# Expert blocks of a hierarchical MoE step: transposes issued one by one between dense products, and results copied out of PSUM by ScalarE

## What is computed

```python
def expert_block(args):
    e, tok = args
    xb = x_pad[tok]                                              # (128, 1024)
    hmid = jax.nn.silu(xb @ w_gate[e]) * (xb @ w_up[e])          # (128, 512)
    return hmid @ w_down[e]                                      # (128, 1024)
```

## Time and profile before

| | us |
|---|---|
| median of 3 runs | 1564.78 (1563.38 to 1565.76) |
| the profiled execution, its time | 1563.39 |
| the profiled execution, its span | 1561.7 |
| expert stage in it, from its first product to the last copy of `yb` | about 912 to 1510 |
| PE busy over the span | 1437.0 (92%) |
| DVE busy | 1076.0 (69%) |
| ACT busy | 783.5 (50%) |
| POOL busy | 555.0 (36%) |
| granted TensorE clock, mean | 0.956 |

### The profile page before, as it was taken

One profiled execution on the slowest core, in us unless ns is written; L12 is line 12 of the kernel. 1 busy time (PEld: TensorE's weight loads), 2 busy tenths in 40 slices (PEclk: granted clock), 3 DMA queues, 4 the chain that ended last, 5 costly groups with the idle time before them and its releaser, 6 DMA issues. The chain is left out here.

```text
span 1561.7 us, 22591 instructions
## 1 busy us (share of the span) xinstructions
PE 1437.0 (92%) x7667; PEld 1246.8 (80%) x7667; DVE 1076.0 (69%) x1414; ACT 783.5 (50%) x1053; POOL 555.0 (36%) x363
## 2 busy tenths in 40 slices
PE   5899999999999998899999559999999999999955
PEld 3899999999999997788777457788888888887842
DVE  4588823166665564544554559999999999999936
ACT  5342223233333433443342418777777777777814
POOL 5423324454444442484554013423333241111111
PEclk8999999999999999899999669999999999999978
DMA  4123332234444445677553639999999999999867
GB/s 176 42 70 96 110 116 83 79 110 156 152 151 154 146 142 188 237 222 238 164 172 111 222 142 368 391 385 382 384 374 375 381 373 378 371 378 372 312 240 292
DMA packets 166995, 360.59 MB, mean 231 GB/s; under 512 B 20948, under 2 KB 50644, under 8 KB 166932
## 3 DMA queue, kind: packets, MB, share of 16 engines
q1 hardware_dynamic: 151364, 321.85, 57.6%
q0 software_dynamic: 15568, 37.87, 7.1%
HBM read 316.00 MB, written 59.64 MB: 241 GB/s over the span
## 5 line engine op out<-in xcount | busy, mean ns | idle before, releaser
L61 PE MATMUL bank<-xh,wh 128*128 128x352 f32 x864 | 295.6, 342 | 5.7 <-ACT raw L885 2.9
L63 PE MATMUL bank<-xh,wl 128*128 128x352 f32 x864 | 279.2, 323 | 0.0
L62 PE MATMUL bank<-xl,wh 128*128 128x352 f32 x864 | 278.7, 323 | 0.0
L1801 POOL DMA_INDIRECT scratch_picked<-yb,dst x32 | 90.9, 2841 | 250.0 <-DVE yb L1974 250.0
L1887 ACT CAST wg_h<-wg 128x1024 fp32r<-128x1024 f32 x124 | 131.1, 1058 | 96.7 <-PE bank L63 61.5
L1980 DVE TENSOR_TENSOR wg_l<-wg,wg_h 128x1024 fp32r<-128x1024 f32 x128 | 156.6, 1223 | 24.8 <-ACT wu_h L1888 23.3
L61 PEld LDWEIGHTS bank<-xh,wh 128*128 128x128 f32 x864 | 163.7, 190 | 10.3 <-issue 5.5
L1639 POOL TENSOR_TENSOR wol<-wo,woh 128x1024 fp32r<-128x1024 f32 x48 | 122.0, 2553 | 126.9 <-ACT woh L972 126.8
L62 PEld LDWEIGHTS bank<-xl,wh 128*128 128x128 f32 x864 | 164.2, 190 | 2.9 <-issue 1.9
L63 PEld LDWEIGHTS bank<-xh,wl 128*128 128x128 f32 x864 | 163.2, 189 | 0.0
L1981 DVE TENSOR_TENSOR wu_l<-wu,wu_h 128x1024 fp32r<-128x1024 f32 x128 | 155.7, 1216 | 0.0
(11 more groups left out here) (382 smaller groups left out, 3259.6 us busy)
## 6 DMA issues: line engine op xcount, KB each, us to landing
wg<-in_w_gate SPq DMA_DIRECT2D x128, 512.0 KB, 6.0
wu<-in_w_up SPq DMA_DIRECT2D x128, 512.0 KB, 11.1
wd<-in_w_down SPq DMA_DIRECT2D x128, 512.0 KB, 11.0
wo<-in_w_out SPq DMA_DIRECT2D x48, 512.0 KB, 4.6
w<-in_w_in_tiles SPq DMA_DIRECT2D x36, 512.0 KB, 4.3
yy<-scratch_picked SPq DMA_DIRECT2D x8, 1024.0 KB, 14.2
scratch_xb<-stage POOLq DMA_DIRECT2D x10, 512.0 KB, 4.0
xb<-scratch_xb SPq DMA_DIRECT2D x8, 640.0 KB, 4.4
```

The costliest lines, as they stand in the source:

```text
L61: nc.tensor.matmul(acc, lh, rh, start=start, stop=False)
L62: nc.tensor.matmul(acc, lh, rl, start=False, stop=False)
L63: return nc.tensor.matmul(acc, ll, rh, start=False, stop=stop)
L1801: pool.indirect_dma_start(out=S["picked"], out_offset=bass.IndirectOffsetOnAxis(ap=dst[:], axis=0), in_=yb[:], in_offset=None, bounds_chec ...
```

## The change

`turn_x` and `turn_hid` are cut into steps of one transpose. Inside the loop `down` takes one transpose of the next x after each of its eight groups of three products, and `gate_up` takes one transpose of the previous block's `hid` after each of its first four groups of six. The order of the loop is now `gate_up(i)` with `turn_hid` of block i - 1 inside it, and `down(i - 1)` with `turn_x` of block i + 1 inside it. Outside the loop the transposes of blocks 0 and 1 and of the last `hid` stay in one row. `unload_y` moves from DVE to ACT, where it stands between `high_down(i)` and `high_hid(i)`.

```diff
@@ -1813,16 +1813,24 @@
 
         @block.tensor
         def _(pe):
-            def turn_x(i):
-                pe.wait_ge(xg_loaded, i * 16 + 16)
-                for half in range(2):
+            def turn_x_step(i, k):
+                half, q = k // 4, k % 4
+                if k == 0:
+                    pe.wait_ge(xg_loaded, i * 16 + 16)
+                if q == 0:
                     wait(pe, xT_done, i * 2 + (half - 1))
-                    for q in range(4):
-                        last = nc.tensor.transpose(bank[4 + half][:, q * P:(q + 1) * P], xg[:, (4 * half + q) * P:(4 * half + q + 1) * P],
-                                                   C["ident"][:])
-                    last.then_inc(xT_psum, 1)
-
-            def gate_up(i):
+                out = nc.tensor.transpose(bank[4 + half][:, q * P:(q + 1) * P], xg[:, k * P:(k + 1) * P], C["ident"][:])
+                if q == 3:
+                    out.then_inc(xT_psum, 1)
+
+            def turn_hid_step(i, f):
+                if f == 0:
+                    pe.wait_ge(hid_ready, i + 1)
+                out = nc.tensor.transpose(bank[6][:, f * P:(f + 1) * P], hid[:, f * P:(f + 1) * P], C["ident"][:])
+                if f == FF // P - 1:
+                    out.then_inc(hT_psum, 1)
+
+            def gate_up(i, turn_hid_of=None):
                 wait(pe, hid_ready, i)
                 for k in range(KT):
                     if k % 2 == 0:
@@ -1834,14 +1842,10 @@
                                              start=(k == 0), stop=(k == KT - 1))
                     if k % 2:
                         last.then_inc(gu_used, 1)
-
-            def turn_hid(i):
-                pe.wait_ge(hid_ready, i + 1)
-                for f in range(FF // P):
-                    last = nc.tensor.transpose(bank[6][:, f * P:(f + 1) * P], hid[:, f * P:(f + 1) * P], C["ident"][:])
-                last.then_inc(hT_psum, 1)
-
-            def down(i):
+                    if turn_hid_of is not None and k < FF // P:
+                        turn_hid_step(turn_hid_of, k)
+
+            def down(i, turn_x_of=None):
                 pe.wait_ge(hT_done, i + 1)
                 wait(pe, y_done, i * 2)
                 for f in range(FF // P):
@@ -1850,8 +1854,10 @@
                         s = slice(n * 512, (n + 1) * 512)
                         last = split_product(nc, bank[2 + n][:, :], (hT_h[:, f, :], hT_l[:, f, :]), (wd_h[:, f, s], wd_l[:, f, s]),
                                              start=(f == 0), stop=(f == FF // P - 1))
-                    last.then_inc(down_used, 1)
-
+                        if n == 1:
+                            last.then_inc(down_used, 1)
+                        if turn_x_of is not None:
+                            turn_x_step(turn_x_of, 2 * f + n)
 
             pe.wait_ge(placed, 1)
             for a in range(N_ASG):
@@ -1862,18 +1868,18 @@
             nc.tensor.matmul(bank[1][0:1, 0:MAXBLK], blk_col[:], C["ident"][0:MAXBLK, 0:MAXBLK], start=True, stop=True).then_inc(blk_psum, 1)
             pe.wait_ge(rows_ready, 1)
             m = blocks_but_three(pe) + 1
-            turn_x(0)
+            for k in range(KT):
+                turn_x_step(0, k)
             gate_up(0)
-            turn_x(1)
-            turn_hid(0)
+            for k in range(KT):
+                turn_x_step(1, k)
             with pe.Fori(1, m + 1) as i:
-                gate_up(i)
-                turn_x(i + 1)
-                down(i - 1)
-                turn_hid(i)
-            gate_up(m + 1)
+                gate_up(i, turn_hid_of=i - 1)
+                down(i - 1, turn_x_of=i + 1)
+            gate_up(m + 1, turn_hid_of=m)
             down(m)
-            turn_hid(m + 1)
+            for f in range(FF // P):
+                turn_hid_step(m + 1, f)
             down(m + 1)
 
         @block.scalar
@@ -1910,23 +1916,33 @@
                 wait(act, down_used, i * 4)
                 nc.scalar.copy(hT_h[:], bank[6][:].rearrange("p (k t) -> p k t", k=4)).then_inc(h_high, 1)
 
+            def unload_y(i):
+                wait(act, y_stored, i * 16)
+                act.wait_ge(down_used, i * 4 + 4)
+                for n in range(2):
+                    nc.scalar.copy(yb[:, n * 512:(n + 1) * 512], bank[2 + n][:, :]).then_inc(y_done, 1)
+
             high_x(0)
             m = blocks_but_three(act) + 1
 
-            def block_of(i):
+            def block_of(i, first=False):
                 high_gate_up(i + 1, range(3))
                 silu(i)
                 high_x(i + 1)
                 high_gate_up(i + 1, range(3, 4))
                 high_down(i)
+                if not first:
+                    unload_y(i - 1)
                 high_hid(i)
 
-            block_of(0)
+            block_of(0, first=True)
             with act.Fori(1, m + 1) as i:
                 block_of(i)
             silu(m + 1)
             high_down(m + 1)
+            unload_y(m)
             high_hid(m + 1)
+            unload_y(m + 1)
 
         @block.vector
         def _(dve):
@@ -1967,12 +1983,6 @@
                 wait(dve, hT_psum, i)
                 nc.vector.tensor_tensor(hid[:], act_g[:], bank[1][:, :], ALU.mult).then_inc(hid_ready, 1)
 
-            def unload_y(i):
-                wait(dve, y_stored, i * 16)
-                dve.wait_ge(down_used, i * 4 + 4)
-                for n in range(2):
-                    nc.vector.tensor_copy(yb[:, n * 512:(n + 1) * 512], bank[2 + n][:, :]).then_inc(y_done, 1)
-
             def low_gate_up(i, pieces):
                 for p in pieces:
                     dve.wait_ge(gu_high, i * 4 + (p + 1))
@@ -2001,24 +2011,20 @@
             low_gate_up(0, range(4))
             low_x(0)
 
-            def block_of(i, first=False):
+            def block_of(i):
                 low_gate_up(i + 1, range(3))
                 gated(i)
                 low_x(i + 1)
                 low_gate_up(i + 1, range(3, 4))
                 low_down(i)
-                if not first:
-                    unload_y(i - 1)
                 low_hid(i)
 
-            block_of(0, first=True)
+            block_of(0)
             with dve.Fori(1, m + 1) as i:
                 block_of(i)
             gated(m + 1)
             low_down(m + 1)
-            unload_y(m)
             low_hid(m + 1)
-            unload_y(m + 1)
 
 
 FIRST = 4
```

## The result

| | before | after |
|---|---|---|
| median of 12 runs each | 1562.22 us (1556.39 to 1565.76) | 1568.12 us (1564.25 to 1570.85) |
| ratio to before, 95% interval | | 1.0035 (1.0023 to 1.0047), +5.5 us |
| span of the profiled execution | 1561.7 | 1566.6 |
| last Silu to the end of the last copies | 19.55 | 17.77 |

A forecast was written before the change was run, and what follows sets the result against it. PE was taken to set 17.71 us a block in mid-stage and late weight loads 18.3 near the end. Order +2.4, gather +1, end -1.1 gave +2.3, so 1567.1 us against 1564.78; range 1561 to 1577.

The forecast's parts named there:

- The transposes on PE: Expert stage, PE: a lone transpose costs 0.12 us, so PE needs 17.75 us a block, 0.04 more than now.
- Rival B: Expert stage, PE: lone transposes at 0.2 us make 18.7 a block, 1587 in all; decides from 0.17 on; chance 0.06.
- The order of the waits: ACT and DVE behind x's last transpose: a chain of 18.3 us makes periods alternate 17.75 and 18.3, +2.4 us.
- G: Start of `gate_up(i + 1)`, right after x's last transpose; the chain through ACT and DVE was timed from it, ending at 18.3.
- The mean: Expert stage: periods of 17.75 and 18.3 average 18.02 us; thirty blocks take 540.6 against 538.2, +2.4 us.
- The loads: Weight loads in the expert stage: the DMA's own pace of 18.0 us a block just fits under 18.02, costing nothing.
- Rival C: Expert stage: the ACT and DVE chain meets weights landing past 13.4 us, +5 to +9, with the gather 1570 to 1575; chance 0.17.
- A: Expert stage: transposes hidden at 0.06 us, the DMA sets the pace; 1563.7, or 1560.7 with the clock held; chance 0.27.
- D: Copies of y on ACT: held by the scatter before last; a 1 us wait per block would be +30; chance 0.02.
- The gather: Gather of x: waits for transposes ending 5.5 us later, leaving 4 us of cover; +1 us, bounds 0 and +4.
- The tail: End of the stage: last `down` 0.9 us earlier, last copies 0.2 shorter, together -1.1; PE's clock 0, bounds 0 and -3.
- The scatter: Scatter of y: copies end on ACT at about G + 7.4, leaving 17 us until the next copies; costs nothing.

The follow-up runs named there:

- e5: The change, with two transposes of x after each of the first four groups of `down`, none after the others: 1562.76 us, ratio 0.9998.
- e7: The change, with a quarter of the columns of each weight load: 1568.63 us, ratio 1.0028.
- e9: The change, with one more 512-column subtraction on DVE per block, 0.6 us, ahead of the hidden rows' low part: 1579.07 us, ratio 1.0093.
- e4: The change, with the copies of y on DVE as before: 1587.97 us, ratio 1.0161.
- e12: e1 with each partition taking two neighbouring rows of `wg` and `wu`, runs of 4 KB for 2 KB: 1557.46 us, ratio 0.9960.
- e1: The kernel before, transposes in rows, with only the copies of y moved to ACT: 1562.24 us, ratio 0.9985.
- e2: The change, with all eight transposes of x in one row ahead of `down`, those of `hid` single: 1561.76 us, ratio 0.9988.
- e10: e1 with one more 0.6 us subtraction on DVE per block: 1562.11 us, ratio 0.9995.
- e13: The change, with partitions taking neighbouring rows of `wg` and `wu` as in e12: 1568.29 us, ratio 1.0032.
- e6: The kernel before, with a quarter of the columns of each weight load: 1555.14 us, ratio 0.9943.
- e8: e1 with a quarter of the columns of each weight load: 1551.97 us, ratio 0.9917.

## Why the prediction was right, and where it was off

1568.1 lies in the range, 1.0 above the 1567.1 predicted. That it lies so close is partly luck: before has a median of 1562.2 over twelve runs, 2.6 below that of the three that the forecast started from, and the same +2.3 from there would have said 1564.5. By difference it is less close: +5.5 us by the ratio, +4.9 by the spans, where the sum said +2.3. The difference went past the 0.2% that the forecast called about what measurement cannot tell from none. The mechanism is the forecast's, as the periods, e5, e7 and e9 show; the size of its main term was less than half of what was measured.

- **The transposes on PE: right in kind, too small.** From the first single transpose of x to the eighth it is 1212.56 - 1206.92 = 5.64 us, 0.806 a step; less three products of 0.227 that is 0.125 each. Those of the hidden rows: (1218.56 - 1214.07) / 3 = 1.497, less six products, 0.135 each. I took 0.12, on the ground that setting them singly changes nothing; it adds 0.01 to 0.02 to the 0.112 of the burst. Eight and four of them make 1.54, and 72 products 16.34, together 17.88, and 17.90 from start to start, for the 17.75 of the forecast; 0.04 of it is that I wrote 16.3 for 16.34. Rival B, from 0.17 on, did not come near. The estimate of 17.0 by the Trainium skill (TensorE: Matmul & The Clock Gate, Part 2) took the page's 56 ns, which it gives for an isolated product; for a stream of weight loads and products the same part gives about 81 ns at 128 columns. Here the transpose costs 112 to 135 ns, above both. With what the page says of weight loads pulled under the running product the trace agrees: in 1008 to 1150.72 after, PEld is busy for 112.6 us and PE for 141.7 of the same 142.7.
- **The order of the waits: right, and confirmed by experiment.** DVE at piece 3 at G + 2.79 (2.7), hidden rows' low part at G + 9.6 (9.5), end of x's first half at G + 18.30, start of the next `gate_up` at G + 18.35 (18.3), every second block, with PE waiting 0.44 (0.55). The wait of one block frees the next one, as said: the transposes of x were in their banks at about 1230.50, and 1230.50 + 18.35 = 1248.85 is where `gate_up` started (1248.86). e9 shows the halving from the other side, and e4 the 19.5 that I gave for a chain with the copies on DVE: 37.48 - 17.90 = 19.58.
- **The mean**: (17.92 + 18.35) / 2 = 18.13 for 18.02, times 30 is +3.4 us. This is the term that was mis-sized, by 0.15 on PE's own period and 0.05 to 0.1 of handovers on the chain; it had +2.4 and measured +5.8. Its bounds held it: I had allowed PE 0.36 more a block, half of it on the mean.
- **The loads: right that they would not bind, in one place wrong in the reading.** That landing times fall from 13.0 to 9.6 is as forecast. But the 18.0 us that I called the DMA's own pace is a pace of these transfers, not of the DMA engines: e12 moves the same bytes at 17.81 a block. And it sets the average of the whole stage before, not only its end (e1, e2, e5 and e10 above).
- **Rival C** had its right half, the chain, and missed on its trigger: landings stayed under 13.4 us (11.0 at most in 1320 to 1360), e7 keeps the time with a third of the traffic, and e13 with longer rows. Its 1570 to 1575 is above what was measured, but by the gather that it counted in and by the lower median of before: the stage's +5.8 lies inside its +5 to +9 and outside the forecast's +2.4. So the time alone does not decide between the two; the alternating periods and e7 do. **A** fell with the transposes' price and with e7; **D** with ACT's waits: no wait of ACT before `yb` in the loop.
- **The gather: +1 came to nothing.** All 32 issues take 1.01 to 1.11 us and land after 7.3 at most, and no transpose in the loop waits for `xg`. The slow issue of the earlier trace rows had gone with one period of 21.71 us before. That period is gone, and to judge by e1, which lacks it too and takes as long, it had cost before nothing in sum.
- **The tail: -1.1 said, -1.8 measured.** -0.87 of it is the last hidden rows' way to `down`, as said (-0.9), and -0.2 the shorter copies, as said. Between them lie two terms that the sum had at nothing. PE's granted clock still fell to 0.50, the level of 1.2 GHz, after an idle time of 2.94 us, but from about 1506.1 to 1509.5, where before it was there from the start of `down` at 1499.74 to about 1505.7. The steps between products are 0.43 us there for 0.23, and from its first to its last product `down` takes 6.9 us for 8.1: -1.2, so the clock was worth something between 0 and -3. Against it the last copies wait for the scatter issued at 1505.01, which lands after 8.3 us; they start 0.98 after the start of PE's last product, for 0.49 before: +0.5. "The scatter: nothing" holds in the loop and not at the end.

The sum by measured terms: +5.8 for 30 blocks and +0.75 for the ends of the pipe (Silu 0 stands 0.24 later, and the first and last blocks make up the rest: the last Silu is at 1496.64 for 1490.09, +6.55), less 1.8 in the tail: +4.8, where the spans differ by 4.9.

Where the room on DVE went: in the old order, with the copies on ACT, DVE has room for 0.6 us more a block at no cost (e10). In the new order DVE stands idle around the second half of x instead, for 0.96 and 1.20 us, in which it waits for ACT and ACT for the last transpose.

## To carry to other kernels

Where a producer's pieces are spread evenly over a phase, the last comes at its end. An in-order consumer stops there with all that is queued behind it, whether that depends on the piece or not. Walk from the last piece through each in-order engine to the next phase that needs them, and compare this time with the period, since busy shares don't tell. If the walk is longer than the producer's own period by d, and a late start does not lengthen the walk, the cost is d / 2 a block. Spread the pieces over the first half (e5), or keep the row.

## What the runs showed of the hardware

**The length of a contiguous run, at equal bytes.** In 1200 to 1300, e1 and then e12:

```profile
DMA packets 16880, 37.62 MB, mean 376 GB/s; under 512 B 2081, under 2 KB 2081, under 8 KB 16880
```

```profile
DMA packets 11245, 37.98 MB, mean 380 GB/s; under 512 B 1975, under 2 KB 1975, under 8 KB 11245
```

A third fewer packets for one percent more bytes. Landing of `wu` in 1320 to 1360 has a median of 12.8 us in e1 and 9.5 in e12, and the periods of 18.3 are gone. A part of that is that PE in e12 asks for a block every 17.81 us and not every 17.71; but e1's loads did not keep up with 17.81 either (near 17.95 over the stage), and those of e12 do. The difference is small, about 1%, and was enough.

**POOL's issue of an indirect DMA** takes 1.04 us or much longer. For the scatter the mean over its 32 issues is 1.04 in the change, 1.91 in e12, 2.84 before, 4.15 in e4 and 5.11 in e6. Groups of the page, of before and of e6:

```profile
L1801 POOL DMA_INDIRECT scratch_picked<-yb,dst x32 | 90.9, 2841 | 250.0 <-DVE yb L1974 250.0
```

```profile
L1801 POOL DMA_INDIRECT scratch_picked<-yb,dst x32 | 163.5, 5109 | 260.2 <-DVE yb L1974 260.2
```

It is not the traffic: e6 has the least and the longest issue. The long ones are those of kernels in which DVE makes the copies of `yb` (2.84, 4.15, 5.11), the short ones those in which ACT does (1.04 to 2.03), and e4 differs from the change in nothing else. The timelines say why the place of the copies could matter. One issue of e4, and DVE beside it:

```profile
1228.01 7.42 POOL L1801 DMA_INDIRECT scratch_picked<-yb,dst  x1 [9.45 <-DVE yb L1980]
```

```profile
1227.64 1.22 DVE L1986 TENSOR_TENSOR wg_l<-wg,wg_h 128x1024 fp32r<-128x1024 f32 x1
...
1233.32 1.22 DVE L1987 TENSOR_TENSOR wu_l<-wu,wu_h 128x1024 fp32r<-128x1024 f32 x1
1234.45 0.68 DVE L1974 TENSOR_TENSOR hid<-act_g,bank 128x512 f32<-128x512 f32 x1
```

The issue begins among six subtractions of DVE with both operands in SBUF that follow each other without a gap. It ends at 1235.43, 0.9 us after the last of them. In before, e1, e4, e5, e6, e8, e10 and e12 all 228 issues, scatters and gathers, that take over 1.3 us end like this: about 0.9 us after the end of such a subtraction, sometimes the last of its run (7.4 us for a whole run, 5.14 where DVE pauses after four), sometimes one in the middle (1.74). The slow gather of the earlier trace rows is one of them. In the change the issue begins at 1220.99, just ahead of the end of one at about 1221.15, and is not stretched. So the length goes by where in DVE's run the issue falls, and the copies on DVE put it at the start of a run. This is read from traces; no run moves DVE's work alone to test it. The issues were covered in all kernels but for the one slow gather of before, so they cost nothing here; they would where the cover is short.
